# Last group of the output projection by token halves, its first half gated ahead, one modulation pair moved behind it

## The reference

```python
mod = silu(c) @ w_ada + b_ada                    # (2048) @ (2048 x 12288)
sh1, sc1, gt1, sh2, sc2, gt2 = split(mod, 6)
h = rms_norm(x, g_norm1) * (1 + sc1) + sh1
a_out, b_out = differential_attention(...), latent_attention(...)   # from h @ w_in
mix = concatenate([a_out, b_out], axis=-1) @ w_out                  # 256 x 2048 @ 2048 x 2048
x = x + gt1 * mix
h2 = rms_norm(x, g_norm2) * (1 + sc2) + sh2
ffn = (silu(h2 @ w_gate) * (h2 @ w_up)) @ w_down
x = x + gt2 * ffn
```

## Time and profile before

| what | us |
| --- | --- |
| median of three runs | 2655.3 |
| the profiled execution | 2656.51 |
| its span | 2654.1 |
| TensorE busy in the span | 2583.4 (97%) |
| VectorE busy | 1547.0 (58%) |
| ScalarE busy | 1166.7 (44%) |
| idle of TensorE ahead of the second norm's first matmul | 7.50 |

### The profile page before, as it was taken

One profiled execution on the slowest core, in us unless ns is written; L12 is line 12 of the kernel. 1 busy time (PEld: TensorE's weight loads), 2 busy tenths in 40 slices (PEclk: granted clock), 3 DMA queues, 4 the chain that ended last, 5 costly groups with the idle time before them and its releaser, 6 DMA issues.

```text
span 2654.1 us, 32740 instructions
## 1 busy us (share of the span) xinstructions
PE 2583.4 (97%) x12054; PEld 2074.6 (78%) x12054; DVE 1547.0 (58%) x1698; ACT 1166.7 (44%) x1522; POOL 54.3 (2%) x86
## 2 busy tenths in 40 slices
PE   7999989899999999999999999999999999999997
PEld 2676766688888888887888888888888888888886
DVE  1456664577776555557655454566555656555555
ACT  2344554344444444444544455444544444444443
POOL 1010110000000000000000000000000000000000
PEclk8999999899999999999999999999999999999999
DMA  9968776657776555555655545566555555555552
GB/s 391 384 231 292 261 270 239 229 199 248 250 249 222 191 191 190 191 191 178 211 191 186 177 153 175 186 202 238 188 193 189 190 190 190 190 190 189 188 189 98
DMA packets 263106, 563.80 MB, mean 212 GB/s; under 512 B 9251, under 2 KB 13525, under 8 KB 261869
## 3 DMA queue, kind: packets, MB, share of 16 engines
q1 hardware_dynamic: 260688, 549.25, 61.0%
q0 software_dynamic: 1952, 11.27, 1.2%
q10 hardware_dynamic: 380, 2.13, 0.2%
HBM read 558.40 MB, written 4.21 MB: 212 GB/s over the span
## 4 chain that ended last, share of the span: by engine, by line
PE 83%; DVE 2%; ACT 1%; issue 0%; DMA 0%; POOL 0%; DVEq 0%; POOLq 0%; ACTq 0%
PE acc L635 79%; PE bank L716 2%; PE bank L665 1%; DVE w_lo L1681 0%; PE acc L857 0%; PE acc L909 0%; PE bank L728 0%; PE bank L866 0%; PE acc L855 0%; DMA raw<-in_w_ada 0%; DVE wide L2191 0%; DVE x_res L2195 0%; PE acc L1067 0%; PE acc L1068 0%; DVE actT_hi L1812 0%
## 5 line engine op out<-in xcount | busy, mean ns | idle before, releaser
L1681 DVE TENSOR_TENSOR w_lo<-raw,w_hi 128x1024 fp32r<-128x1024 f32 x852 | 1037.7, 1224 | 831.1 <-ACT w_hi L1153 802.3
L1153 ACT ACTIVATE w_hi<-raw 128x1024 fp32r<-128x1024 f32 x852 | 902.8, 1062 | 1059.0 <-PE acc L635 948.8
L635 PE MATMUL acc<-w_hi,actT_hi 128*128 128x512 f32 (+1 forms) x2112 | 833.7, 395 | 2.0 <-DVE actT_lo L1814 0.8
L635 PE MATMUL acc<-w_hi,actT_lo 128*128 128x512 f32 (+1 forms) x2112 | 821.8, 389 | 0.0
L635 PE MATMUL acc<-w_lo,actT_hi 128*128 128x512 f32 (+1 forms) x2112 | 821.4, 389 | 0.0
L635 PE MATMUL acc<-w_hi,mixT_hi 128*128 128x512 f32 (+1 forms) x1280 | 504.1, 394 | 9.6 <-DVE mixT_lo L1804 5.4
L635 PE MATMUL acc<-w_hi,mixT_lo 128*128 128x512 f32 (+1 forms) x1280 | 497.6, 389 | 0.0
L635 PE MATMUL acc<-w_lo,mixT_hi 128*128 128x512 f32 (+1 forms) x1280 | 497.2, 388 | 0.0
L635 PEld LDWEIGHTS acc<-w_hi,actT_hi 128*128 128x128 f32 x2112 | 397.6, 188 | 108.5 <-issue 21.7
L635 PEld LDWEIGHTS acc<-w_hi,actT_lo 128*128 128x128 f32 x2112 | 397.4, 188 | 82.6
L635 PEld LDWEIGHTS acc<-w_lo,actT_hi 128*128 128x128 f32 x2112 | 397.8, 188 | 79.6 <-issue 1.0
(11 more groups left out here) (275 smaller groups left out, 1066.9 us busy)
## 6 DMA issues: line engine op xcount, KB each, us to landing
raw<-in_w_ff SPq DMA_DIRECT2D x128, 1024.0 KB, 5.1
raw<-in_w_in SPq DMA_DIRECT2D x108, 1024.0 KB, 5.2
raw<-in_w_ada SPq DMA_DIRECT2D x64, 1024.0 KB, 5.2
raw<-in_w_gate SPq DMA_DIRECT2D x44, 1024.0 KB, 5.1
raw<-in_w_up SPq DMA_DIRECT2D x44, 1024.0 KB, 5.1
raw<-in_w_down SPq DMA_DIRECT2D x44, 1024.0 KB, 5.0
early_mix<-in_w_ada SPq DMA_DIRECT2D x16, 1024.0 KB, 8.8
wide<-in_w_ada SPq DMA_DIRECT2D x16, 1024.0 KB, 8.7
```

The lines of the kernel that those rows point to most:

```text
L635: last_mm = pe.matmul(acc[p][:, t, 0:width], act[x][:, k0 + c, t * P:(t + 1) * P], w[:, u % SPL, c * NW:c * NW + width], start=first and c ...
L1153: act.activation(w_hi[:, u % SPL, :], raw[:, ld % RAW, (u % DU) * 1024:(u % DU + 1) * 1024], ACT.Copy) \
L1681: dve.tensor_tensor(w_lo[:, u % SPL, :], raw[:, ld % RAW, (u % DU) * 1024:(u % DU + 1) * 1024], w_hi[:, u % SPL, :].bitcast(F32), ALU.subt ...
```

## The change

Four edits go together.

(a) The last group (units 104 to 107) is multiplied by token halves: all 24 matmuls of t = 0 over the four units first, then the 24 of t = 1. The places of the rings are given back only in the second pass.

(b) In all four groups the parked first half is gated and added to `x_res` ahead of the group's end (behind VectorE's second split of the group; in group 0 behind the third, in the last behind the first). Behind the sum there remain one product with the gate and one addition; in the last group these are done for each token half as soon as its pass has ended, on 512 columns of one half each. VectorE's splits of units 108 and 109 stand between the two halves, that of unit 110 behind the diagonal; ScalarE sums the squares of t = 0, makes `w_hi` of 108 and 109, and then sums those of t = 1.

(c) The places of the pairs: 23 pairs instead of 24 over the 39 loads from the 13th on, and the last pair behind the last load of `w_out`. It is multiplied behind unit 107, between the last matmul of the projection and the norm's first.

(d) The order of the groups: both row groups of gt1 come ahead of the second group of sc2, which is now the last. Its columns are made behind unit 109, and ScalarE waits for them only at the fifth pair of chunks.

```diff
-GAPS = [0] * 12 + [2 * ((i + 1) * 24 // 39 - i * 24 // 39) for i in range(39)] + [0] * 3
+GAPS = [0] * 12 + [2 * ((i + 1) * 23 // 39 - i * 23 // 39) for i in range(39)] + [0, 0, 2]
+LAST_OUT = 2 * len(GAPS) - 1
-... for kind, pair in ((3, 0), (4, 0), (3, 1), (4, 1), (2, 0), (2, 1))]
+... for kind, pair in ((3, 0), (4, 0), (3, 1), (2, 0), (2, 1), (4, 1))]
 # modulation(), products(v)
+        if v == LAST_OUT:
+            after = [len(GAPS) - 1]
+        elif v % DU or after == [len(GAPS) - 1]:
+            after = []
 # TensorE
-            for g in range(4):
+            for g in range(3):
                 group(g % 2, MIXT, 8, k0=8, ...)
+            def group_by_halves(p, act, k0, n):
...
+                for t in range(TT):
+                    for j in range(n):
+                        if t == 0:
+                            pe.wait_ge(lo_ready, L.next("unit"))
+                        for c in range(UC):
+                            for s, (x, w) in enumerate(((0, w_hi), (0, w_lo), (1, w_hi))):
+                                ins = pe.matmul(acc[p][:, t, :], ...)
+                        if t == 1:
+                            ins.then_inc(unit_used, 1)
+                    if t == 0:
+                        ins.then_inc(half_summed, 1)
+            group_by_halves(1, MIXT, 8, 4)
+            modulate()
             normT(0, 4)
 # ScalarE
+            unit()
+            group_sums(2)
+            act.wait_ge(half_ready, 1)
+            last_sums(0)
+            units(2)
+            act.wait_ge(xg_ready, L.next("xg"))
+            last_sums(1).then_inc(xg_summed, 1)
+            act.wait_ge(xg_summed, L.n["xg"])
+            unit()
-            act.wait_ge(mod_ready, len(PROLOGUE) + 4)
+            act.wait_ge(mod_ready, len(PROLOGUE) + 2)
 # VectorE
+            def gated_to(dst, src, g):
+                gate_ = grow[:, g * NW:(g + 1) * NW].unsqueeze(1).broadcast_to([P, TT, NW])
+                link(dve.tensor_tensor(dst, src, gate_, ALU.mult))
+            def add_first_half(g):
+                if g == 0:
+                    dve.wait_ge(xb_in, 16)
+                gated_to(wide[:, :, cols], wide[:, :, cols], g)
+                link(dve.tensor_tensor(x_res[:, :, cols], x_res[:, :, cols], wide[:, :, cols], ALU.add))
+            for g in range(3):
+                at = {1: lambda g=g: add_first_half(g)}          # g == 0: at the third unit
+                units(4, at)
                 sum_ready()
-                link(dve.tensor_tensor(s3, acc[g % 2][:, :, :], wide[:, :, cols], ALU.add))
+                gated_to(s3, acc[g % 2][:, :, :], g)
                 free(g % 2)
-                for t in range(TT):
-                    ins = dve.tensor_tensor(s3[:, t, :], s3[:, t, :], grow[:, cols], ALU.mult)
                 link(dve.tensor_tensor(x_res[:, :, cols], x_res[:, :, cols], s3, ALU.add))
                 group_ready()
+            def add_half(t):
+                link(dve.tensor_tensor(s3[:, t, :], acc[1][:, t, :], grow[:, cols], ALU.mult))
+                link(dve.tensor_tensor(x_res[:, t, cols], x_res[:, t, cols], s3[:, t, :], ALU.add))
+            last_unit()
+            add_first_half(3)
+            dve.wait_ge(half_summed, 1)
+            add_half(0)
+            dve.sem_inc(half_ready, 1)
+            last_unit()
+            last_unit()
+            L.next("unit")
+            sum_ready()
+            add_half(1)
+            free(1)
+            group_ready()
+            modulated_here()
             diagonal(x_inv_rms())
+            split()
```

More of the change, by code:

```diff
@@ L77 @@
 PROLOGUE = [(kind, k0, n) for k0, n in SEGMENTS for kind in (0, 1)]
-GROUPS = PROLOGUE + [(kind, 8 * pair, 8) for kind, pair in ((3, 0), (4, 0), (3, 1), (4, 1), (2, 0), (2, 1))]
+GROUPS = PROLOGUE + [(kind, 8 * pair, 8) for kind, pair in ((3, 0), (4, 0), (3, 1), (2, 0), (2, 1), (4, 1))]
 LOAD_OF = [(g, r) for g, (kind, k0, n) in enumerate(GROUPS) for r in range(n)]
@@ L133, in products @@
         after = [0, 1] if v == 0 else [v // DU + 1]
-        return [NPRO + LOADS_A.index(k) for j in after if v >= 0 and v % DU == 0 and j < len(LOADS_W) - 1
+        if v == LAST_OUT:
+            after = [len(GAPS) - 1]
+        elif v % DU or after == [len(GAPS) - 1]:
+            after = []
+        return [NPRO + LOADS_A.index(k) for j in after if v >= 0 and j < len(LOADS_W) - 1
                 for k in range(LOADS_W[j] + 1, LOADS_W[j + 1])]
@@ L139, in early @@
         return [LEAD + 1 + v] if 0 <= v < NPRO - LEAD - 1 else []
-    events = [("row" if n >= len(PROLOGUE) + 4 else "columns", n) for a in products(u - 2) for n in completed(a)]
+    events = [("row" if n >= len(GROUPS) or GROUPS[n][0] == 2 else "columns", n)
+              for a in products(u - 2) for n in completed(a)]
     events += [("columns", n) for a in early(u - 1) for n in completed(a)]
@@ L356, in build @@
         xg_ready = sem("xg_ready")
+        half_summed = sem("half_summed")
+        half_ready = sem("half_ready")
         xg_summed = sem("xg_summed")
@@ L927, in _ @@
                 unit((u // 4) % 2, MIXT, UC * (u % 4), u % 4 == 0, u % 4 == 3, todo=window(52 + u) + heads_at(u))
-            for g in range(4):
+            for g in range(3):
                 at = {j: lambda j=j: run(heads_at(16 + j)) for j in range(3)} if g == 0 else None
                 group(g % 2, MIXT, 8, k0=8, at=at, ready=(lambda j: outputs_taken(H + UC * j)) if g == 0 else None)
+            def group_by_halves(p, act, k0, n):
+                u0, m = L.n["unit"], L.n[("acc", p)]
+                L.next(("acc", p))
+                pe.wait_ge(acc_free[p], m)
+                for t in range(TT):
[4 more added lines that the diff above has]
+                            for s, (x, w) in enumerate(((0, w_hi), (0, w_lo), (1, w_hi))):
+                                ins = pe.matmul(acc[p][:, t, :], act[x][:, k0 + UC * j + c, t * P:(t + 1) * P],
+                                                w[:, (u0 + j) % SPL, c * NW:(c + 1) * NW],
+                                                start=j == 0 and c == 0 and s == 0,
+                                                stop=j == n - 1 and c == UC - 1 and s == 2)
+                        if t == 1:
[4 more added lines that the diff above has]
+            modulate()
             normT(0, 4)
@@ L1415, in _, with last_sums, scaled2 @@
                     at = {0: lambda g=g: group_sums(g - 1)}
-                units(4, at)
-            group_sums(3)
-            act.wait_ge(mod_ready, len(PROLOGUE) + 4)
+                if g < 3:
+                    units(4, at)
+            unit()
+            group_sums(2)
+            def last_sums(t):
+                return act.activation(sq[:, t * NW:(t + 1) * NW], x_res[:, t, 3 * NW:D], ACT.Square,
+                                      accum_out=ssx[:, t, 3:4])
+            act.wait_ge(half_ready, 1)
[6 more added lines that the diff above has]
+            act.wait_ge(mod_ready, len(PROLOGUE) + 2)
             for k in range(2):
+                scaled(k, mcol[:, 4, :], mcol[:, 3, :])
+            def scaled2(k):
+                if k == 4:
+                    act.wait_ge(mod_ready, len(PROLOGUE) + 4)
                 scaled(k, mcol[:, 4, :], mcol[:, 3, :])
@@ L1432, in _ @@
             L.n["stg"] = 4 + 2 + 4 + 4
-            units(16, {**{j: lambda j=j: scaled(j + 2, mcol[:, 4, :], mcol[:, 3, :]) for j in range(6)},
+            units(16, {**{j: lambda j=j: scaled2(j + 2) for j in range(6)},
                        7: lambda: silu_gate(first=True)})
@@ L1694, in unit, with modulated_here @@
                 run(todo)
+                modulated_here()
+            def modulated_here():
                 for what, n_ in modulation(L.n["unit"] - 1):
@@ L1766, in part_row @@
                         dve.wait_ge(gt1_bias, 16)
-                        at_ = (2 * (n_ - len(PROLOGUE) - 4) + j) * NW
+                        at_ = GROUPS[n_][1] * P + j * NW
                         dst, sums = grow[:, at_:at_ + NW], bank[b][:, :]
@@ L2128, in _ @@
                 unit(window(52 + u) + heads_at(u))
-            for g in range(4):
-                units(4, {j: lambda j=j: run(heads_at(16 + j)) for j in range(3)} if g == 0 else None)
+            s3 = stg.rearrange("p (t n) -> p t n", t=TT)
+            def gated_to(dst, src, g):
+                gate_ = grow[:, g * NW:(g + 1) * NW].unsqueeze(1).broadcast_to([P, TT, NW])
+                link(dve.tensor_tensor(dst, src, gate_, ALU.mult))
+            def add_first_half(g):
                 if g == 0:
@@ L2133, in _ @@
                     dve.wait_ge(xb_in, 16)
+                cols = slice(g * NW, (g + 1) * NW)
+                gated_to(wide[:, :, cols], wide[:, :, cols], g)
[3 more added lines that the diff above has]
+                if g == 0:
+                    at = {0: lambda: run(heads_at(16)), 1: lambda: run(heads_at(17)),
+                          2: lambda: [run(heads_at(18)), add_first_half(0)]}
+                units(4, at)
@@ L2143, in _, with last_unit @@
```

(7 more changed lines are left out.)

2 lines of the change are left out of this document (removed).

## The result

The changed kernel takes 2665.98 us (median of 8 runs, 2664.78 to 2668.23), the kernel before in the same session 2655.71 (8 runs, 2654.34 to 2660.18): ratio 1.0036, 95% interval 1.0025 to 1.0046. It is slower by 0.25% to 0.46%. The prediction said 2651.6, from 2647.5 to 2656.0.

What follows compares the result with a forecast made beforehand. TensorE, busy 97% of the span, was taken as the bound. From 2655.3 us, -2.2 (place), -0.8 (neighbouring pairs) and -0.7 (clock) sum to -3.7, giving 2651.6 us, range 2647.5 to 2656.0.

Steps and rivals of the forecast that it cites:

- the moved pairs among the narrow units: Units of 316 to 376 us, where TensorE waits for others' chains: sign unread, adds nothing, range 1.5 us wider either side.
- rival B: Gain lost in moved pairs (one more 2.8 us wait) or first pass (2.74 us): -1 in all, 2654.3 us; chance 0.14.
- Pair behind unit 107, row moved ahead, shift of -0.9 by unit 96: Ahead of unit 96 TensorE loses a pair and a column group, gains a gt1 row: -0.9 us; late pair costs nothing.
- Neighbouring pairs, -0.8: Input projection: one fewer neighbourhood where a second pair waits for its load; -1.0 at best, 0 at least, -0.8 us taken.
- The stall in the first pass, 1.25: Last group's first pass: TensorE wants unit 107 at 503.8 but stands until 505.05 for VectorE's split, 1.25 us.
- The last end work 1.7 us late: Projection's end: second half's end work starts 1.7 us after TensorE has ended, two splits being ahead of it on VectorE.
- Idle time 4.4 us: In front of the norm's first matmul: TensorE idle for 4.4 us (513.8 to 518.2) instead of 7.50.
- The product with the gate read twice: VectorE's 1024-column gating product at group ends: taken from above as two halves, 1.31 us, 1.37 with the link.
- Rival C: Slower: VectorE bounds the groups if the gate product takes twice its 1.23 us; 7.2 against -3.7, 2658.8 us; chance 0.06.
- The clock behind the norm, -0.7: Norm and unit 108: shorter idle may keep TensorE's clock up, between 0 and -3.0 us; -0.7 taken.
- the columns, +0.8: Modulation columns moved from ahead of unit 96 to behind unit 109, where TensorE is the bound: +0.8 us there.
- Nothing given back later: From unit 108 on: TensorE runs without a gap, a 7 us later DMA queue has 14 us to spare; no loss.

Runs made afterwards that it cites:

- the first hybrid: Full change with its own pair places up to unit 52 and those of the kernel before from unit 54 on: 2653.55 us, ratio 0.9987 to the kernel before.
- the ends alone: Kernel before with only the passes by token halves and the first half gated ahead, pairs and group order unchanged: 2654.59 us, ratio 0.9989.

## Why the prediction was wrong, step by step

- **The step that failed** is the sentence on the moved pairs among the narrow units: "its sign I can't read, so it widens the range by 1.5 on either side and adds nothing". From unit 58 to unit 97 the changed kernel loses 12.9 us, against the -0.9 (one pair and one group of columns less, one row more) that I had for the stretch. I had the row that showed the danger, 2.81 us at 356.63, and priced one more such wait at 2.8 us in rival B, which had the mechanism but not its size. There were five new ones of over 2 us (2.64, 2.14, 2.62, 2.27, 2.06), at four places, and the lower clock came at each: the idle time grew by 6.3 us, the slower work by some 7.8. The range's 1.5 us was too small by far. Moving three pairs by one place brought the time back to that of the kernel before. I should have laid each of the nine new places beside the heads' work in the trace and asked which bank the pair would need there.
- **That TensorE's clock falls there too** was in none of my terms. For the gap at the norm I set that of 2.81 us, which it survived, as a measure, and for this stretch I priced idle time alone. In the changed kernel the clock is at the lower level from 296.7 on, behind an idle time of 1.29 us and inside that of 2.64; the pair of 363.11 behind 2.80 us still has its 1.92 us, as has its counterpart in rows 5; in the one with three pairs moved the same pair takes 3.52 us behind the same 2.80. The wait of 3.25 us at 1255 has both outcomes too, and one of 3.36 us in the first hybrid left the clock up. So the length of one gap doesn't decide it. The Trainium skill ("TensorE: Matmul & The Clock Gate", "A second HAM failure mode: psum-queue depth-cycling") describes that short idle times between groups of matmuls, where PSUM banks are cycled, make the clock swing between its two levels; the rows at 297 to 301 and 343 to 347 agree in that the lower level stands there beside waits of 2.64 and 2.62 us for a bank. They don't tell when it comes.
- **Pair behind unit 107, row moved ahead, shift of -0.9 by unit 96:** right where nothing disturbs it: the first hybrid goes from -0.4 at unit 58 to -1.2 at unit 97. The pair's loads were there, and its products lie beside VectorE's work.
- **Neighbouring pairs, -0.8:** -0.5 by unit 58. Further on the neighbours 76 and 78, with a row between, cost 2.06.
- **The stall in the first pass, 1.25:** 0.87, and 0.84 to 0.90 in every other kernel with that order and the pair behind unit 107; with the ends alone there is none.
- **The last end work 1.7 us late:** TensorE's pair starts at 523.77, right behind the projection, and the end work at 524.65 (VectorE's timeline; the chain counts it from 524.74): 0.9 late. The mechanism is the one of the walk: ScalarE's first `w_hi` is ready at 522.35, and both of VectorE's splits go ahead of the end work.
- **Idle time 4.4 us:** 3.52. From TensorE's start at the stalled unit to the norm I had 518.2 - 505.05 = 13.15 us; measured 529.22 - 516.73 = 12.49.
- **The product with the gate read twice:** 1.22 us, as a plain one (from above I had 1.31). Rival C's ground fell away, though its sign came true by another mechanism.
- **The clock behind the norm, -0.7, and the columns, +0.8:** from the norm to 577 us the shift goes from 8.9 to 7.9. It falls by 1.9 over unit 108 (first matmuls of units 108 and 109: +8.85 and +6.99), and the columns behind unit 109 take 0.9 back. The lower level lasted 3.4 us instead of 13.7; the term was too small by over 1 us.
- **Nothing given back later:** 1.6 us at 1255, where the clock fell behind a wait that both kernels have.

The first hybrid is what the forecast described, the change's ends with pairs that don't hit the heads: ratio 0.9987 (0.9977 to 0.9996), where the forecast was 2651.6 / 2655.3 = 0.9986. That the two meet so closely is luck: the interval is 5 us wide, at the norm the trace stands at -4.6 where the forecast had -3.8, single terms were off by up to 1.6 us, and 1.8 us lie between that trace and the median. The mechanism that I worked out was real and of the size that I said, and was outweighed nearly threefold (4.5 us given back, 12.9 lost) by a term that I had set to zero.

## What to carry to other kernels

When a constant in a spreading formula changes (24 pairs over 39 places to 23), many items move, not only the one that is meant: here 11 of the 23 that stay, nine of them to places that had no pair. Compare the lists of places before costing anything, and hold each new place against the waits and the banks in use there. An in-order engine pays twice for such a wait, once idle and once at the lower clock; here the two were of about one size (6.3 and 7.8 us). A term whose sign can't be read, in a stretch with 2 to 3 us waits, needs a range of several such waits.

## What the runs showed of the hardware

- A GpSimd operation on 128x2 elements took 0.19 us beside an idle VectorE and 1.08 us beside a VectorE operation with two inputs in SBUF, ending when that ended (516.01 against 515.97). The Trainium skill ("SBUF — State Buffer", "Who interferes with whom") states that the two share a pair of ports as an exclusive lock; the rows agree. What looks like a free slot, VectorE waiting for GpSimd, wasn't one here.
- A pair of products took 1.92 us at the upper level and between 3.4 and 3.8 at the lower; one idle time of 2.80 us stood before the first kind in one kernel and before the second in another. One of 3.25 us for the same `mixT_lo` was followed by 3.4 us at the lower level in the changed kernel and by none in the kernel before.
- How often the clock falls between 290 and 410 us differs among kernels that compute the same with pairs one place apart: 23.9 us at the lower level in the changed kernel, 3.4 in the first hybrid. What exactly decides it in a given stretch stayed open.
